# Column-group reads in a gated recurrence, attention combined pair by pair, and both results turned in halves

## What is computed

```
# layer 0 of the second block: 8 heads, chunks of 32 tokens, 8 chunks
def step(state, xs):
    q_c, k_c, v_c, dec = xs
    o_c = einsum('bchk,bhkv->bchv', q_c, state)          # read the state
    state = dec * state + einsum('bchk,bchv->bhkv', k_c, v_c)   # grow it
    return state, o_c
o = o_intra + o_inter
o = o * rsqrt(mean(o * o, axis=-1) + eps) * norm_g       # per head
o = o * silu(g);  y = o @ w_out

# layer 1: three groups of dilated attention g = 0, 1, 2, 8 heads each
p = exp(s - m); z = sum(p); o_g = p @ v / z; lse_g = m + log(z)
wts = softmax(stack(lse), axis=0)                        # over the 3 groups
o = sum_g wts[g] * o_g;  y = o @ w_out
```

## Time and profile before

| | |
|---|---|
| median of three runs | 2974.56 us |
| the profiled execution's own time | 2975.61 us |
| its span | 2973.8 us |
| PE, PE weight load busy | 2802.6 us (94%), 2396.3 us (81%) |
| DVE, ACT, POOL busy | 1132.4 us, 475.6 us, 173.6 us |
| PE busy in tenths, 40 slices | 8999899999999999999999999798799799996998 |

### The profile page before, as it was taken

The page is one execution under the profiler, slowest core; times in us unless marked ns, Lnnn a source line. Parts: engine busy times, 40 slices in busy tenths (PEclk is TensorE's granted clock), DMA queues, the critical chain, the costliest instruction groups (busy, mean ns, idle before and its releaser), DMA issues.

```text
span 2973.8 us, 37216 instructions
## 1 busy us (share of the span) xinstructions
PE 2802.6 (94%) x16494; PEld 2396.3 (81%) x16494; DVE 1132.4 (38%) x1583; ACT 475.6 (16%) x741; POOL 173.6 (6%) x154
## 2 busy tenths in 40 slices
PE   8999899999999999999999999798799799996998
PEld 5768788998586888899988877576699778765997
DVE  5443324664544232533320000426455532235332
ACT  1251111001135110100000000122210101121101
POOL 0002210000001220000000000000000011000000
PEclk9999999999999999999999999899799899997999
DMA  7432125776443212344547888433377544321441
GB/s 256 142 126 78 66 72 204 262 272 234 144 153 114 72 57 75 142 149 156 176 164 254 271 275 284 141 116 111 114 276 289 192 143 141 128 99 57 162 172 64
DMA packets 211952, 476.10 MB, mean 160 GB/s; under 512 B 7632, under 2 KB 36944, under 8 KB 211536
## 3 DMA queue, kind: packets, MB, share of 16 engines
q1 hardware_dynamic: 211216, 472.26, 46.0%
q10 hardware_dynamic: 576, 1.46, 0.1%
HBM read 472.64 MB, written 1.05 MB: 159 GB/s over the span
## 4 chain that ended last, share of the span: by engine, by line
PE 82%; issue 10%; DVE 4%; ACT 2%; DMA 1%; POOL 1%; SPq 0%; POOLq 0%; DVEq 0%; ACTq 0%
PE ps L450 28%; PE ps L1566 16%; PE ps L1707 9%; PE ps L1894 7%; PE ps L503 6%; PE ps L1923 3%; PE ps L462 3%; PE ps L1080 1%; PE ps L1091 1%; PE ps L1087 1%; PE ps L1933 1%; PE ps L2327 0%; PE ps L1866 0%; PE ps L700 0%; DVE h L2277 0%
## 5 line engine op out<-in xcount | busy, mean ns | idle before, releaser
L450 PE MATMUL ps<-uT,ring 128*128 128x256 f32 x2816 | 631.4, 383 | 21.7 <-DMA ring<-in_w_in 10.0
L450 PEld LDWEIGHTS ps<-uT,ring 128*128 128x128 f32 x2816 | 537.1, 193 | 99.2 <-issue 15.8
L1707 PE MATMUL ps<-work,ring 128*128 128x256 f32 x1584 | 345.7, 379 | 0.0
L1707 PEld LDWEIGHTS ps<-work,ring 128*128 128x128 f32 x1584 | 299.2, 190 | 39.7
L1894 PEld LDWEIGHTS ps<-work,ring 128*128 128x128 f32 x1760 | 198.6, 192 | 5.1 <-issue 4.8
L1894 PE MATMUL ps<-work,ring 128*128 128x128 f32 (+4 forms) x1760 | 198.4, 275 | 0.0
L1566 PE MATMUL ps<-uT,ring 128*128 128x128 f32 x1584 | 190.9, 280 | 3.2 <-ACT uT L823 2.5
L1566 PEld LDWEIGHTS ps<-uT,ring 128*128 128x128 f32 x1584 | 188.0, 197 | 6.3 <-issue 5.3
L450 PE MATMUL ps<-xn,ring 128*128 128x256 f32 x768 | 175.2, 387 | 9.5 <-issue 6.9
L1566 PE MATMUL ps<-xn,work 128*128 128x128 f32 x1584 | 179.8, 275 | 0.0
L1566 PEld LDWEIGHTS ps<-xn,work 128*128 128x128 f32 x1584 | 178.3, 192 | 0.0
(11 more groups left out here) (385 smaller groups left out, 3311.6 us busy)
## 6 DMA issues: line engine op xcount, KB each, us to landing
ring<-in_w_in SPq DMA_DIRECT2D x72, 1024.0 KB, 5.1
work<-in_ada_w SPq DMA_DIRECT2D x48, 1024.0 KB, 10.0
ring<-in_exp_w_down SPq DMA_DIRECT2D x40, 1024.0 KB, 5.0
ring<-in_attn_w_in SPq DMA_DIRECT2D x36, 1024.0 KB, 5.1
ring<-in_exp_w_gate SPq DMA_DIRECT2D x32, 1024.0 KB, 6.0
ring<-in_exp_w_up SPq DMA_DIRECT2D x32, 1024.0 KB, 6.7
ring<-in_ffn_w_in SPq DMA_DIRECT2D x32, 1024.0 KB, 6.5
ring<-in_ffn_w_out SPq DMA_DIRECT2D x20, 1024.0 KB, 5.1
```

The source lines that it names most:

```text
L450: mm = pe.matmul(acc[:, m * T:(m + 1) * T], w[:, k, m * P:(m + 1) * P], src[:, half * 4 + k, :], start=(half == 0 and k == 0 and m % 2 == ...
L1707: mm = pe.matmul(bank[2 + n // 4][:, n % 4 * T:(n % 4 + 1) * T], w[:, k, n * P:(n + 1) * P], hid[g][:, t0 + k, :], start=False, stop=True, ...
```

## The change

The recurrence: `across` takes a range of chunks and goes through the heads outside and the chunks inside, so that neighbouring products have different column groups. It runs once for chunks 1 to 3 and once for 4 to 7. The sums of squares of `ho0` are put before the last `state`, its gate after it. `ho1` is normed in two halves, in a buffer of its own, and turned by `halves_pe`.

```diff
-            for c in range(1, NC):
-                across(c)
-                if c + 1 < NC - 1:
-                    grow_state(c + 1)
+            for c in range(2, 4):
+                grow_state(c)
+            across(1, 4)
+            for c in range(4, NC - 1):
+                grow_state(c)
+            across(4, NC)
...
+            def across(c0, c1):
+                t = c0 // 4
+                acc = ps[slot_of[f"ho{t}"]]
+                pe.wait_ge(hg_s, c1 - 1)
+                for n in range(GH):
+                    for c in range(c0, c1):
+                        r = HG_C * (c % 4)
+                        mm = pe.matmul(acc[r:r + HG_C, n * P:(n + 1) * P], hq[:, n, c * HG_C:(c + 1) * HG_C],
+                                       S[c][:, n, :], start=False, stop=True, skip_group_check=True, tile_position=(0, r))
...
-            turn_pe(pe, "so0", hg)
...
+            halves_pe(pe, "so0", hg, hg_lo, 1, "ho", "wo", oT, early=True)
...
-            for c in range(NC - 1):
+            for c in range(NC - 2):
                 state(c)
-            head_norm_dve(dve, 4, "ho0", ...)
-            head_norm_dve(dve, 5, "ho1", ...)
-            turn_dve(dve, "so0", oT, col("hgng"))
+            head_sums(4, 0, 0, GH)
+            state(NC - 2)
+            head_gate(4, 0, 0, GH, None)
+            head_sums(5, 1, 0, HALF)
+            head_sums(6, 1, HALF, GH)
+            head_gate(5, 1, 0, HALF, hg_lo)
+            head_gate(6, 1, HALF, GH, nat_ready)
+            turn_hi_dve(dve, "so0", oT, col("hgng"))
```

```diff
+            def pair_exponents(j):                       # DVE, behind "s" of group 2
+                ... two minima of 128x4, then 128x12 ALU.subtract into w_pair(wg, j)
+            def pair_weights(j):                         # DVE, at "t" of group 2
+                ... six operations of 4 to 12 columns, the reciprocal among them
+                for g in range(2):
+                    o = pair_of(ao[g], j)                # 128x512
+                    i_ = dve.tensor_tensor(o, o, w4(wg[...]).broadcast_to([P, TT, 2, P]), ALU.mult)
+                dstep(dve, dve.tensor_tensor(pair_of(ao[0], j), pair_of(ao[0], j), pair_of(ao[1], j), ALU.add))
...
                 elif what == "o":
+                    if g == 2:
+                        dve.wait_ge(at_o, 2 * PAIRS + j + 1)
+                        i_ = dve.tensor_tensor(pair_of(ao[0], j), pair_of(ao[0], j), pair_of(ao[2], j), ALU.add)
+                        if j % 2:
+                            i_.then_inc(tick(nat_ready if j == 3 else at_lo), 1)
...
+                    if g == 2:                           # ACT, behind the exponentials of "s"
+                        act.wait_ge(at_part, j + 2)
+                        act.activation(w_pair(wg, j), w_pair(wg, j), ACT.Exp).then_inc(tick(at_lse), 1)
-            turn_pe(pe, "so1", ao[0])
...
+            halves_pe(pe, "so1", ao[0], at_lo, 1, "ao", "wao", oT, early=True)
```

More of the change, by code:

```diff
@@ L201, in build @@
         ada_in, ada_sum = [sem(f"ada_in{i}") for i in range(4)], sem("ada_sum")
[L202 to L207, removed]
+        hg_q, hg_f, hg_lb, hg_ff, hg_ln, hg_b, hg_exp, hg_mul, hg_nat, hg_a, hg_s, hg_lo = (
+            sem(n) for n in ("hg_q", "hg_f", "hg_lb", "hg_ff", "hg_ln", "hg_b", "hg_exp", "hg_mul", "hg_nat", "hg_a", "hg_s", "hg_lo"))
+        at_v, at_s, at_p, at_t, at_o, at_lse, at_lo, at_part = (
+            sem(n) for n in ("at_v", "at_s", "at_p", "at_t", "at_o", "at_lse", "at_lo", "at_part"))
+        y_zero, gate_row, ple_out, plg_out, hg_v, hg_gt, tab_sin = (
+            sem(n) for n in ("y_zero", "gate_row", "ple_out", "plg_out", "hg_v", "hg_gt", "tab_sin"))
         up_phase, snap_out, quad_out, w_sum, t_sum = (
@@ L2396, in hgrn_act @@
                 act_sq = full(act, f"ho{t}")
[L2397 to L2400, removed]
+                for part in ((0, 1024),) if t == 0 else ((0, 512), (512, 1024)):
+                    act.activation(hsq2[t][:, part[0]:part[1]], act_sq[:, part[0]:part[1]], ACT.Square).then_inc(tick(hn_sq), 1)
+            turn_lo_act(act, "so0", oT, col("hgng"))
             post_act(act, "spost0", ["wo0", "wo1"], grow)
@@ L2471, in state, with head_sums, head_gate @@
                 dve.wait_ge(hg_s, c + 1)
-            for c in range(NC - 1):
-                state(c)
[L2475 to L2478, removed]
-            turn_dve(dve, "so0", oT, col("hgng"))
+            def head_sums(n, t, h0, h1):
+                k = hcol[n]
+                dve.wait_ge(hn_sq, n + 1)
+                dstep(dve, dve.tensor_reduce(hsum[:, k:k + h1 - h0], hsq2[t][:, h0 * P:h1 * P].rearrange("p (n c) -> p n c", c=P), AX, ALU.add))
+                dve.tensor_scalar(hms[:, k:k + h1 - h0], hsum[:, k:k + h1 - h0], 1.0 / P, EPS, ALU.mult, ALU.add).then_inc(tick(hn_ms), 1)
+            def head_gate(n, t, h0, h1, ready):
+                k = hcol[n]
+                dve.wait_ge(hn_rs, n + 1)
+                acc = full(dve, f"ho{t}")
+                heads = lambda x: x[:, h0 * P:h1 * P].rearrange("p (n c) -> p n c", c=P)
+                i_ = dve.tensor_tensor(heads(hsq2[t]), heads(acc), hrs[:, k:k + h1 - h0].unsqueeze(2).broadcast_to([P, h1 - h0, P]), ALU.mult)
+                dstep(dve, i_)
+                if h1 == GH:
+                    free(f"ho{t}")
+                dve.wait_ge(hg_gt, 1)
+                i_ = dve.tensor_tensor(hg[:, t, h0 * P:h1 * P], hg[:, t, h0 * P:h1 * P], hsq2[t][:, h0 * P:h1 * P], ALU.mult)
+                dstep(dve, i_)
+                if ready is not None:
+                    dve.nop().then_inc(tick(ready), 1)
+            for c in range(NC - 2):
+                state(c)
+            head_sums(4, 0, 0, GH)
[6 more added lines that the diff above has]
+            turn_hi_dve(dve, "so0", oT, col("hgng"))
             for part in range(2):
@@ L2492, in build, with w_pair @@
         xf_ = xn.rearrange("p t d -> p (t d)")
-        nmx, zs, lse, rz, wg = (xf_[:, 1536 + 48 * k:1584 + 48 * k] for k in range(5))
+        nmx, zs, rz, wg = (xf_[:, 1536 + 48 * k:1584 + 48 * k] for k in range(4))
         mx3, wsum = (xf_[:, 1792 + 16 * k:1808 + 16 * k] for k in range(2))
+        def w_pair(x, j):
+            return x.rearrange("p (g n) -> p g n", g=3)[:, :, 4 * j:4 * j + 4]
         ss = [area(18, 768).rearrange("p (n c) -> p n c", n=2), area(21, 768).rearrange("p (n c) -> p n c", n=2)]
@@ L2599, in attn_act @@
                     free(unit)
[L2600 to L2604, removed]
+            turn_lo_act(act, "so1", oT, ones[:, 0:8])
             post_act(act, "spost1", ["wao0", "wao1"], grow)
@@ L2645, in attn_dve @@
                     dve.tensor_reduce(nv[:, 1, :], v[:, :, P:384], AX, ALU.max, negate=True).then_inc(tick(at_s), 1)
+                    if g == 2:
+                        pair_exponents(j)
+                elif what == "t" and g == 2:
+                    pair_weights(j)
                 elif what == "o":
@@ L2653, in attn_dve @@
                     dst = ao[g][:, :, j * 256:(j + 1) * 256].rearrange("p t (n c) -> p t n c", c=P)
-                    dve.tensor_tensor(dst, src, w4(rz[:, c:c + 4]).broadcast_to([P, TT, 2, P]), ALU.mult).then_inc(tick(at_o), 1)
+                    i_ = dve.tensor_tensor(dst, src, w4((wg if g == 2 else rz)[:, c:c + 4]).broadcast_to([P, TT, 2, P]), ALU.mult)
+                    i_.then_inc(tick(at_o), 1)
                     free(unit)
[L2657 to L2674, removed]
+                    if g == 2:
+                        dve.wait_ge(at_o, 2 * PAIRS + j + 1)
+                        i_ = dve.tensor_tensor(pair_of(ao[0], j), pair_of(ao[0], j), pair_of(ao[2], j), ALU.add)
+                        if j % 2:
+                            i_.then_inc(tick(nat_ready if j == 3 else at_lo), 1)
+            turn_hi_dve(dve, "so1", oT, ones[:, 0:8])
             for part in range(2):
```

58 lines of the change are left out of this document (37 added, 21 removed).

## The result

The changed kernel takes 2955.12 us (median of four, 2949.64 to 2956.40), the one before on the same chip 2973.66: ratio 0.9933, 95% interval 0.9921 to 0.9945, 18.5 us faster (0.67%). 2957.4 was forecast, and a range of 2949 to 2968. The profiled execution took 2955.03 with a span of 2953.2, against 2975.61 and 2973.8.

A forecast was written before the change was run, and what follows sets the result against it. PE was taken to bound the kernel (82% of the chain that ended last), both output products waiting for other engines. Gains of 6.9 us in the recurrence and 10.3 in attention sum to 17.2: 2957.4 us, range 2949 to 2968.

The forecast's parts named there:

- Bound and places: Whole kernel: PE bounds it; gains come only where both output products wait for other engines, 16.06 and 19.5 us.
- Two at a time: Recurrence reads: two streams on different column groups overlap, so the runs take 2.9 and 3.7 us at full clock.
- rival 2: Recurrence reads: four streams at once, 1.6 and 2.0 us at full clock; 2953.8 us, chance 0.15.
- Clock of the recurrence: Last reads, after 4.5 us of PE idle: partly at 1.2 GHz, taking 5.6 us, between 3.7 and 7.4.
- X: Recurrence: the end of the last reads, forecast at 2075.4, 0.4 us later than before.
- X to product: Recurrence, last reads' end to output product: 7.75 us; product starts at 2083.2, 7.9 earlier.
- The slack behind the product: Behind the recurrence's product start: feed-forward sums end at 24.3 us, DVE's first sum of squares follows at 24.9; no cost.
- Attention: Group 2 to output product: pairwise work starts the product 11.2 us earlier, minus 0.95 for upper transposes: 10.3 us gained.
- The halves: Both output products: eight transposes ahead of each, the upper half's eight inside it at 0.95 us.
- Rivals 1, 3, 4: 1 (0.28): no reads overlap, 2964.0; 3 (0.10): DVE waits for ACT's exponential, 2963.4; 4 (0.05): group changes empty array, 2985.5.
- rival 1: Recurrence reads: nothing overlaps between column groups, recurrence gains 0.3 us; 2964.0 us, chance 0.28.

The follow-up runs named there:

- e6: Changed kernel with reads spread: chunks 1 and 2 together, 3, 4, 5 and 6 together, 7 alone, between updates; 2949.84 us.
- e7: Changed kernel with the sums of ho0's squares behind the last state again; 2952.65 us.
- e9: As e6 with one run of reads less: chunks 1 and 2, 3, 4 to 6, then 7 alone; 2951.11 us.
- e2: Changed kernel with the recurrence as before, so only attention changed; 2961.64 us.
- e4: Changed kernel with both results turned whole and both output products column half by column half as before; 2961.65 us.
- e3: Changed kernel with chunk as outer and head as inner loop in each run of reads, so neighbouring products stay on one column group; 2957.87 us.
- e10: Changed kernel with the products inside chunks 4 to 7 moved from behind the first two updates to just ahead of the first reads; 2954.75 us.
- e5: Changed kernel with reads of one chunk at a time between the updates, as before; 2953.63 us.
- e8: From e5: ho0's sums one state earlier, its scaling between the last two states, last read marks its first four heads; 2952.69 us.
- e12: The e6 kernel once more, unchanged, over five runs; 2949.96 us.

## Why the prediction was right, and where it was not

- **Bound and places: right.** All the time came from the two stretches that the earlier trace rows showed, and nothing came back behind them.
- **"Two at a time": wrong.** As many streams run as there are column groups. A run of reads takes 1.93 us at full clock for one chunk, 1.94 for two (e6), 1.95 for three (e7, 48 reads), and at half clock 3.62 for one (e9) and 3.64 for four. So the second instruction of a product does not hold up the next product's first, as I had it. For the overlap rival 2 was right. Its 1.6 us for the first reads was a slip, though: it divides 48 instructions by four, and chunks 1 to 3 have only three groups, so 16 x 0.11 + 0.2 = 2.0 was the bound. The Trainium skill (TensorE: Matmul & The Clock Gate, "Measured speedup vs the span model") gives 2.38 times for three column tiles of 512 columns; with 128 columns, three runs of 1.93 against one of 1.95 are 3.0 times in this case's traces, and the measurement decides.
- **Clock of the recurrence: right in kind, wrong in place.** I had the fall in front of the last reads. It came at the first reads, and updates 4 to 6 took 10.2 us at half clock where I had 6.5 (2058.8 to 2065.3). The last state ended 25.7 us behind the first update instead of 24.1, and the last reads took 3.64 instead of 5.6. The two errors cancel: X was forecast 29.7 us behind the first update (2075.4), and is 29.4. A right sum of two wrong terms, which is luck. It also means that the column groups, which I let cost 0.4 us in all, neither gained nor lost anything at X in this trace.
- **X to product: right.** 7.75 forecast, 2083.31 - 2075.33 = 7.98 measured; POOL's two powers over 4 columns took 1.98, 0.99 each, for 1.01 by the line between two rows. The stage gained 6.6 us where 6.9 was forecast.
- **The slack behind the product: right, barely.** The feed-forward sums did end 24.6 us behind its start and the first sum of squares followed at 25.1 (forecast 24.3 and 24.9).

```profile
2105.62 2.29 DVE L1639 TENSOR_TENSOR work<-ring,work 128x2048 f32<-128x2048 f32 x1 [0.95 <-DMA ring<-in_ffn_w_in]
...
2108.42 0.69 DVE L671 TENSOR_TENSOR work<-work 128x512 f32<-128x512 f32 x1 [0.51 <-ACT work L665]
```

- **Attention: mechanism right, size short by 3.7.** 10.3 forecast, 14.0 measured. DVE reached the lower half's signal in 2670.68 - 2648.12 = 22.6 us for my 23.2. The term mis-sized is the clock: I put PE nearer to half clock up to the transposes (40.14 - 11.2 = 28.9 us from mask to product, measured 27.15), which is 1.8; PE's last transposes and products of group 2 took 5.1 us (2667.45 to 2672.53) of the 3.5 to 6.6 that I had bounded them by, and the lower transposes ran at full clock in 1.04 instead of 1.95. And I had the product begin at half clock, as before. It began at full clock: from product to statistics 30.82 + 0.95 = 31.8 was forecast and 29.83 measured, 1.9 more. e2 has the same, while e4 lost it again (its 128 instructions take 29.41).
- **The halves: right for attention, not for the recurrence.** e4 shows 7.5 us of stage in attention and nothing in the recurrence. There the product starts 2.8 us earlier, but its first 32 instructions take 9.33 us instead of the 7.14 of full clock, as the clock is at 0.50 for a little over 4 us of them.
- **Rivals 1, 3, 4: out.** The reads overlap (e3 comes nearest to what rival 1 describes); DVE never waited for ACT's small exponential (from the first mask of group 2 to the last sum its operations follow each other without a wait); 56 changes of group cost nothing that shows.

## What to carry to other kernels

A faster piece on TensorE gains nothing by itself when its neighbours come to run at half clock, as the updates here did: look at the granted clock of the neighbours before counting the gain. Whether the gaps it leaves or the new order brought the clock down was not isolated here. Split work that stands serially behind the last producer (here the softmax and its scalings) into the steps in which that engine waits; that was 6.5 of 14.0 us here, and the halves, added to it, were the other 7.5. Where several stages vary from run to run, compare a stage from its own first instruction.

## What the runs showed of the hardware

- Products on different column groups run side by side at no cost that shows: 1.93, 1.94 and 1.95 us for one, two and three groups at full clock, 3.62 and 3.64 for one and four at half clock.
- The granted clock fell to 0.50 also while PE was issuing without a pause: in e10 inside updates of 32 of 128 rows, in e9 in full products right behind two such updates. It stayed there through 10.2 us of updates in the changed kernel; where updates 4 to 6 alternated with reads (before, e5, e6, e8, e12), it stayed at 1.00 up to the last read. The cause is not isolated.
- The start of the first update, behind identical programs, lies between 2042.1 and 2045.9 us. So differences under 4 us between single executions of this kernel say nothing.
